# Seven block products in another order, and the weight sums waited for one at a time

## What is computed

```python
x = x + mix @ lp["w_out"]
h = rms_norm(x, lp["norm_ffn"])
x = x + (jax.nn.silu(h @ lp["w_gate"]) * (h @ lp["w_up"])) @ lp["w_down"]
x = x + jax.nn.sigmoid(rms_norm(x, lp["norm_ple"]) @ lp["w_ple_gate"]) * (pe @ lp["w_ple_proj"])
```

## Time and profile before

| | us |
|---|---|
| median of 3 runs | 1913.64 (1911.23 to 1916.33) |
| profiled execution, its own time | 1916.08 |
| span of the profiled execution | 1914.3 |
| PE busy | 1750.2 (91%) |
| DVE busy | 1378.9 (72%) |
| ACT busy | 749.6 (39%) |
| POOL busy | 648.9 (34%) |
| granted TensorE clock, mean | 0.972 |

### The profile page before, as it was taken

One profiled execution on the slowest core, in us unless ns is written; L12 is line 12 of the kernel. 1 busy time (PEld: TensorE's weight loads), 2 busy tenths in 40 slices (PEclk: granted clock), 3 DMA queues, 4 the chain that ended last, 5 costly groups with the idle time before them and its releaser, 6 DMA issues.

```text
span 1914.3 us, 31306 instructions
## 1 busy us (share of the span) xinstructions
PE 1750.2 (91%) x10796; PEld 1522.2 (80%) x10796; DVE 1378.9 (72%) x2307; ACT 749.6 (39%) x1555; POOL 648.9 (34%) x437
## 2 busy tenths in 40 slices
PE   7999899999999989889899999999799998998998
PEld 6998786677888888677788888888588788887777
DVE  5466884765888888655688778877877777676643
ACT  5212455545444444534443334334344344343211
POOL 2204692212554555412622322232334324331000
PEclk9999997999999999999899999999899999999999
DMA  6300000011322222110222312231122312323011
GB/s 204 99 31 16 10 1 1 1 46 44 117 67 64 57 53 80 39 56 1 89 73 81 110 66 80 73 110 66 45 89 88 110 66 89 108 66 137 29 36 47
DMA packets 112122, 126.56 MB, mean 66 GB/s; under 512 B 25923, under 2 KB 98144, under 8 KB 112013
## 3 DMA queue, kind: packets, MB, share of 16 engines
q1 hardware_dynamic: 110019, 124.23, 20.3%
q10 hardware_dynamic: 2002, 1.03, 0.2%
HBM read 119.33 MB, written 6.26 MB: 66 GB/s over the span
## 4 chain that ended last, share of the span: by engine, by line
PE 46%; issue 19%; DVE 16%; POOL 11%; ACT 4%; SPq 3%; DMA 1%; DVEq 0%; POOLq 0%; ACTq 0%
PE ps L2239 11%; PE ps L2240 11%; PE ps L2241 11%; POOL arena L966 2%; POOL stats L813 2%; POOL w_raw L967 2%; POOL arena L969 2%; PE ps L2648 2%; DVE arena L2077 1%; DVE arena L1599 1%; PE ps L569 1%; DVE w_lo L1965 1%; PE ps L2481 1%; DVE arena L2133 1%; SPq L671 1%
## 5 line engine op out<-in xcount | busy, mean ns | idle before, releaser
L2239 PE MATMUL ps<-t_hi,w_hi 128*128 128x288 f32 (+1 forms) x1232 | 359.4, 292 | 13.6 <-DVE arena L2077 6.1
L2241 PE MATMUL ps<-t_hi,w_lo 128*128 128x288 f32 (+1 forms) x1232 | 358.1, 291 | 0.0
L2240 PE MATMUL ps<-t_lo,w_hi 128*128 128x288 f32 (+1 forms) x1232 | 357.9, 290 | 0.0
L2239 PEld LDWEIGHTS ps<-t_hi,w_hi 128*128 128x128 f32 x1232 | 235.3, 191 | 18.5 <-DVE w_lo L1965 6.8
L966 POOL TENSOR_TENSOR arena<-w_raw 128x512 f32<-128x512 f32 x44 | 74.0, 1682 | 501.1 <-DVE w_lo L1965 501.1
L2240 PEld LDWEIGHTS ps<-t_lo,w_hi 128*128 128x128 f32 x1232 | 235.3, 191 | 0.9
L2241 PEld LDWEIGHTS ps<-t_hi,w_lo 128*128 128x128 f32 x1232 | 235.3, 191 | 0.0
L976 POOL TENSOR_TENSOR arena<-arena,mhalf 128x32 f32<-128x32 f32 x32 | 177.1, 5534 | 144.1 <-DVE arena L1978 144.1
L2143 DVE TENSOR_TENSOR arena<-arena,ps 128x512 f32<-128x512 f32 x187 | 127.0, 686 | 112.1 <-PE ps L2241 109.5
L2239 PE MATMUL ps<-wd_hi,a_hi 128*128 128x512 f32 x352 | 148.3, 421 | 36.9 <-DVE wd_lo L2065 26.1
L2239 PE MATMUL ps<-cw_hi,pT_hi 128*128 128x288 f32 x512 | 161.1, 315 | 10.2 <-DVE pT_lo L1880 9.4
(11 more groups left out here) (341 smaller groups left out, 4301.2 us busy)
## 6 DMA issues: line engine op xcount, KB each, us to landing
w_raw<-in_w_gate SPq DMA_DIRECT2D x22, 1024.0 KB, 5.3
w_raw<-in_w_up SPq DMA_DIRECT2D x22, 1024.0 KB, 5.4
arena<-in_cache_ckv SPq DMA_DIRECT2D x128, 128.0 KB, 2.0
w_uk<-in_w_down SPq DMA_DIRECT2D x22, 512.0 KB, 3.5
w_uv<-in_w_down SPq DMA_DIRECT2D x22, 512.0 KB, 4.4
arena<-in_x_prompt SPq DMA_DIRECT2D x16, 512.0 KB, 5.4
gw_raw<-in_w_in SPq DMA_DIRECT2D x8, 512.0 KB, 6.0
w_out<-in_w_out SPq DMA_DIRECT2D x1, 4096.0 KB, 13.4
```

Source lines behind the costliest of these rows:

```text
L2239: mm(out, left[0], right[0], start=start, stop=False)
L2240: mm(out, left[0], right[1], start=False, stop=False)
L2241: return mm(out, left[1], right[0], start=False, stop=stop)
```

## The change

- Products are made in the order 0, 3, 6, 1, 4, 2, 5: the three with plain weight quarters first. PRODUCT_BANK is one table for gate units and another for up units, and PE waits for a bank of the last unit place by place instead of for all of the last unit's sums before its second product.
- POOL waits place by place too: w_diff and the sum in place may start when the low part of quarter 1 of the unit before is made (place 4 of 7), w_back after that of quarter 2 (place 6), w_rest after that of quarter 5 (place 7).
- ACT and DVE follow the new order. Per unit the same 7 high parts, 7 low parts, 7 additions, and per group the same pieces of w_down and of the result are made; only their places move. Both first pieces of w_down come early in the unit, the additions of products 2, 1, 6, 4, 4 and 5 come at its end, and the low part of the first result piece comes before them.
- Result pieces are made by token halves. The down products start after two of the four, and wait for the others before the fifth down product. In half 0 the sample tokens' down product is the fifth and no longer the first, and SP loads the next w_down after the fifth down product and no longer after the first.
- All four token sums of half 0 are made after the loop over the output projection; before, three were made within it. In the last unit of each half all four pieces of w_down are split early.
- Buffers of the split weights and tokens move. The output tiles at the end are taken in the order 4, 5, 6, 7, 0, 1, 2, 3, sample tile, where the sample tile was fifth.

```diff
-DOWN_ORDER = ([(TILES, 0)] + [(t, h) for t in range(4, TILES) for h in range(2)], [(t, h) for t in range(4) for h in range(2)])
+DOWN_ORDER = ([(t, h) for t in (4, 5) for h in range(2)] + [(TILES, 0)] + [(t, h) for t in (6, 7) for h in range(2)], [(t, h) for t in range(4) for h in range(2)])
 DOWNS = [len(o) for o in DOWN_ORDER]
 PRODUCTS = 7
-DONE_AT = {0: 1, 2: 2, 3: 3, 1: 4, 4: 5, 5: 6, 6: 7}
-TOKEN_AT = {0: 1, 3: 2, 1: 3, 2: 4, 4: 5, 5: 6, 6: 7}
-PRODUCT_BANK = {0: 0, 2: 1, 3: 2, 1: 3, 4: 4, 5: 5, 6: 1}
+DONE_AT = {0: 1, 3: 2, 6: 3, 1: 4, 4: 5, 2: 6, 5: 7}
+TOKEN_AT = {0: 1, 3: 2, 1: 3, 6: 4, 4: 5, 2: 6, 5: 7}
+PRODUCT_BANK = ({0: 0, 3: 1, 6: 2, 1: 3, 4: 4, 2: 5, 5: 1}, {0: 0, 3: 5, 6: 2, 1: 3, 4: 4, 2: 1, 5: 5})
+OUT_AT = (((0, 0), 1), ((1, 0), 4), ((1, 1), 5), ((0, 1), 7))
...
-END_TILES = [4, 5, 6, 7, TILES, 0, 1, 2, 3]
+END_TILES = [4, 5, 6, 7, 0, 1, 2, 3, TILES]
...
-                        sp.wait_ge(s_("dn_done"), down_at(0, wd_g) + 1)
+                        sp.wait_ge(s_("dn_done"), down_at(0, wd_g) + 5)
...
-                if isinstance(done, int) and done == 0:
+                first = isinstance(done, int) and done == 0
+                if first:
                     pool.wait_ge(s_("m_xT"), NT)
                 else:
-                    pool.wait_ge(s_("w_split"), PRODUCTS * done)
+                    pool.wait_ge(s_("w_split"), PRODUCTS * (done - 1) + DONE_AT[1])
                 nc.gpsimd.tensor_tensor(w_diff, w_part(u, 0), w_part(u, 4), ALU.subtract).then_inc(s_("w_pool"), 1)
                 nc.gpsimd.tensor_tensor(w_part(u, 4), w_part(u, 4), w_part(u, 6), ALU.add).then_inc(s_("w_pool"), 1)
                 pool.wait_ge(s_("w_pool"), w_sum(c, g, u, 2))
+                if not first:
+                    pool.wait_ge(s_("w_split"), PRODUCTS * (done - 1) + DONE_AT[2])
                 nc.gpsimd.tensor_tensor(w_back, w_part(u, 4), w_part(u, 0), ALU.subtract).then_inc(s_("w_pool"), 1)
                 pool.wait_ge(s_("w_pool"), w_sum(c, g, u, 3))
+                if not first:
+                    pool.wait_ge(s_("w_split"), PRODUCTS * done)
                 nc.gpsimd.tensor_tensor(w_rest, w_part(u, 3), w_back, ALU.subtract).then_inc(s_("w_pool"), 1)
...
-            token_sums(0, (4,))
+            token_sums(0, (1, 2, 3, 4))
...
                 act.wait_ge(s_("prod_done"), PRODUCTS * k + DONE_AT[0])
                 if not first:
-                    act.wait_ge(s_("sum_ready"), 7 * k)
-                    if u == 0:
-                        act.wait_ge(s_("glu_ready"), NU + 4 * (g + GROUPS * c))
-                nc.scalar.activation(p_one[:, 0:n], ps[:, PRODUCT_BANK[0], 0:n], ACT.Copy).then_inc(s_("part_copied"), 1)
-                if following:
-                    high_w(*following, 0)
-                if wd:
+                    act.wait_ge(s_("sum_ready"), 7 * (k - 1) + 2)
+                nc.scalar.activation(p_one[:, 0:n], ps[:, PRODUCT_BANK[u][0], 0:n], ACT.Copy).then_inc(s_("part_copied"), 1)
+                high(0)
+                if wd and len(wd[2]) != 2:
+                    high_wd(*wd)
+                elif wd:
                     high_wd(*wd[0:2], wd[2][0:1])
-                if following:
-                    high_w(*following, 2)
-                    high_w(*following, 3)
+                high(3)
+                if wd and len(wd[2]) == 2:
+                    high_wd(*wd[0:2], wd[2][1:2])
+                silu(0)
+                high(6)
                 if turn is not None:
                     scale_turn(turn)
-                if following:
-                    high_w(*following, 1)
-                silu(0, 0, 2)
-                if wd:
-                    high_wd(*wd[0:2], wd[2][1:2])
-                if following:
-                    high_w(*following, 4)
-                silu(1, 1, 4)
-                if following:
-                    high_w(*following, 5)
-                silu(0, 1, 6)
-                if following:
-                    high_w(*following, 6)
-                silu(1, 0, 7)
-                if u == 1:
-                    if c == 1 and isinstance(g, int) and g == 0:
-                        act.wait_ge(s_("dn_done"), down_at(0, GROUPS))
-                    elif not (c == 0 and isinstance(g, int) and g == 0):
-                        act.wait_ge(s_("dn_done"), down_at(c, g))
-                    for j, (f, h) in enumerate(((0, 0), (1, 1), (0, 1), (1, 0))):
-                        act.wait_ge(s_("glu_ready"), NU + 4 * (g + GROUPS * c) + j + 1)
-                        nc.scalar.activation(a_hi_r[f][:, h * n:(h + 1) * n], gate_s[:, f, h * n:(h + 1) * n], ACT.Copy).then_inc(s_("act_high"), 1)
+                high(1)
+                high_a(0)
+                high(4)
+                high(2)
+                for j in (1, 2):
+                    silu(j)
+                    high_a(j)
+                high(5)
+                silu(3)
+                high_a(3)
...
+                low(0)
+                if wd and len(wd[2]) != 2:
+                    low_wd(*wd)
+                elif wd:
                     low_wd(*wd[0:2], wd[2][0:1])
-                if 0 in gains:
-                    gain_h(*gains[0])
-                dve.wait_ge(s_("part_copied"), k + 1)
                 if not (isinstance(k, int) and k == 0):
                     dve.wait_ge(s_("sum_ready"), 7 * k)
                     dve.wait_ge(s_("glu_ready"), NU + 4 * G)
-                add(p_two, p_one, 2, 1, 0)
-                if following:
-                    low_w(*following, 2)
                 if u == 0 and not first:
                     dve.wait_ge(s_("aT_ready"), 4 * G)
                 if u == 1:
                     dve.wait_ge(s_("silu_ready"), 4 * G + 4)
-                add(out_of(0, 0, p_one), p_one, 3, 2, 1)
-                if following:
-                    low_w(*following, 3)
-                mult(0, 0, p_one, 2)
-                add(p_three, p_two, 1, 3, 1)
-                if following:
-                    low_w(*following, 1)
-                if wd:
+                dve.wait_ge(s_("part_copied"), k + 1)
+                add(out_of(0, c_sum), p_one, 3, 1, 0)
+                low(3)
+                mult(0, c_sum)
+                if wd and len(wd[2]) == 2:
                     low_wd(*wd[0:2], wd[2][1:2])
-                add(out_of(1, 1, c_sum), p_three, 4, 4, 3)
-                add(p_two, p_two, 4, 5, 3)
-                mult(1, 1, c_sum, 4)
-                if following:
-                    low_w(*following, 4)
+                if 0 in gains:
+                    gain_h(*gains[0])
+                low(6)
+                low(1)
+                low_a(0)
+                low(4)
                 if 1 in gains:
                     gain_h(*gains[1])
-                add(out_of(0, 1, p_two), p_two, 5, 6, 5)
-                if following:
-                    low_w(*following, 5)
-                mult(0, 1, p_two, 6)
-                add(out_of(1, 0, p_three), p_three, 6, 7, 4)
-                if following:
-                    low_w(*following, 6)
-                mult(1, 0, p_three, 7)
-                if u == 1:
-                    if c == 0:
-                        dve.wait_ge(s_("glu_ready"), NU + 4 * G + 3)
-                        for f in range(2):
-                            ch.link(nc.vector.tensor_copy(a_s[f], gate_s[:, f, 2 * n - NS:2 * n]))
-                    for j, (f, h) in enumerate(((0, 0), (1, 1), (0, 1), (1, 0))):
-                        dve.wait_ge(s_("act_high"), 2 * NT + 4 * G + j + 1)
-                        w = slice(h * n, (h + 1) * n)
-                        nc.vector.tensor_tensor(a_lo_r[f][:, w], gate_s[:, f, w], a_hi[f][:, w], ALU.subtract).then_inc(s_("aT_ready"), 1)
+                add(p_two, p_one, 2, 2, 0)
+                add(p_three, p_two, 1, 3, 2)
+                if u:
+                    dve.wait_ge(s_("glu_ready"), NU + 4 * G + 1)
+                add(out_of(1, c_sum), p_three, 6, 4, 3)
+                low(2)
+                add(out_of(2, p_three), p_three, 4, 5, 4)
+                mult(1, c_sum)
+                add(p_two, p_two, 4, 6, 3)
+                mult(2, p_three)
+                add(out_of(3, p_two), p_two, 5, 7, 6)
+                low(5)
+                mult(3, p_two)
+                if u == 1 and c == 0:
+                    dve.wait_ge(s_("glu_ready"), NU + 4 * G + 4)
+                    for f in range(2):
+                        ch.link(nc.vector.tensor_copy(a_s[f], gate_s[:, f, 2 * n - NS:2 * n]))
+                for j in (1, 2, 3):
+                    low_a(j)
...
-                if not (fixed and m == 0):
-                    pe.wait_ge(s_("sum_ready"), 7 * (m - 1) + 2)
+                start = fixed and m == 0
+
+                def freed(place):
+                    if not start:
+                        pe.wait_ge(s_("sum_ready"), 7 * (m - 1) + place)
+                if not start:
+                    pe.wait_ge(s_("part_copied"), m)
                 product(0)
                 if turns:
```

(20 more changed lines are left out.)

118 lines of the change are left out of this document (68 added, 50 removed).

## The result

The changed kernel takes **1980.82 us** (median of 4 runs, 1978.62 to 1984.16), the kernel before 1913.2 (1911.23 to 1916.33). The ratio is **1.035, 95% interval 1.033 to 1.038**: slower, as forecast, but by 67.6 us where 36 were forecast, and outside the range of 1888 to 1970.

The account below looks back on a forecast made before the run. Bound: DVE's queue from the up unit's tail to the first down_add, lengthened by POOL. Half 0 +21, half 1 +17.5, start +2, ends -4 make +36.5 on 1916.08: 1952.6, median 2.4 lower, so 1950 us; range 1888 to 1970.

Parts of the forecast that it names:

- term for the clock: Both loops: 12 of 20 stalls followed by a half-clock stretch, at 1.7 us each; 1.0 us per group, 0 to 1.7.
- term for the stall: PE's wait for the first down_add per group: 3.85 us against 2.75 in half 0, 4.65 against 3.9 in half 1.
- The bound: DVE's queue from the up unit's tail to the first down_add, lengthened about 4.3 us by POOL's four sums.
- ideal periods: A group's time from PE's matmuls alone in the kernel before: 35.3 us in half 0, 31.2 in half 1.
- The race with POOL: End of the gate unit: POOL's w_back, first by 0.2 us, holds DVE's low part 5, costing 1.2 us per group.
- rival 1: End of the gate unit: DVE goes first, low part 5 isn't held, 1.2 us less per group; about 1919 us; chance 0.20.
- The blocks in the tail: Up unit's tail: w_back before a multiplication adds 1.0 us to DVE's queue, w_rest before the first copy 1.1.
- Start and ends: Start, before the first down products: +2 us (-3 to +6); ends of the halves: together -4 (0 to -6).
- Rival 2: DVE's queue isn't full, as POOL's earlier sums meet additions and idle time; about 1880 us; chance 0.20.
- Rival 3: PE stalls inside units too, if the up unit's tail is 2 us longer; 1975 to 1990 us; chance 0.05.
- Rival 4: POOL's sums stay held by the loads and the order alone acts; about 1915 to 1930 us; chance 0.05.

Follow-up runs that it names:

- filled kernel: The changed kernel with 16 extra, unread matmuls between the second and third down product of the groups in both loops; 1951.7 us.
- The release of POOL as before: The changed kernel with POOL making its four weight sums again only when all seven low parts of the unit are made; 1980.8 us.

## Why the prediction was right, and where it fell short

The sum failed in the size of its terms and not in its direction. Its term for the clock (12 of 20 stalls followed by a stretch, 1.0 us per group) measured 1.83 and 1.57, with a stretch behind all 19 stalls. Its term for the stall (1.1 and 0.75 us more per group than before) measured 2.2 and 1.5. And the last gate unit of half 0 took 8 us more than forecast, with a wait for ACT in it that the sum put at nothing.

**The bound.** Right for the changed kernel. It named DVE's queue from the up unit's tail to the first down_add, and moving four low parts out of it moved the wait one for one. For the kernel before it was half right: "all of it follows from one date, the end of that down_add" is not so. With 2.4 us taken out ahead of that down_add the periods fell by 1.1 us only, because the last w_down piece, in the same queue but further ahead, was a second date that PE waited for (16.2 us in half 1's loop); only with that piece moved too did they fall by 1.4 and 2.8. The ideal periods were right to 0.3 us. What it undersold is POOL: it gave the four sums 4.3 us of DVE's time in a queue with a loss of 2.75 and 3.9, and did not draw the conclusion that without them nothing would be lost at all.

**The stall.** The mechanism was right, its price too small. Laid out: up unit's tail at 18.8, first down_add done at 28.9, stall 3.85 in half 0. Measured: 19.4, 29.6, and PE goes on 4.06 us later than it could (1057.17 to 1061.23). So the stall itself was nearly right, and what comes on top of it was too small. With the clock held up by the extra matmuls, the period rose by 40.30 - 38.07 = 2.2 in half 0, where 1.1 was forecast, and by 1.5 in half 1, where 0.75 was. Against the kernel before without its sums, which has no wait at all, the filled kernel's down products take 17.44 us and not 13.15 in half 0 (a stall of 4.3, 3.85 laid out), and 15.49 and not 11.30 in half 1 (4.2, as laid out). Its two units take 22.86 and not 22.41 us in half 0, and 21.06 and not 19.98 in half 1: 0.45 and 1.1 of waiting for the first addition, laid out as nothing and 0.5. In half 0 a further 0.25 is the ideal period, 35.3 against 35.56 measured: the 2.75 lost before was counted from it, the 3.85 was not.

One cause can be named. An addition that takes the result of the one just before waits for its semaphore, and starts 0.55 us after it and not 0.37: three take 1.59 us, where 0.45 + 2 x 0.37 = 1.19 was laid out. In half 1 two take 0.94 us, where 0.42 + 0.335 = 0.76 was. The change makes five such pairs per group, together 0.9 us, two of them in the up unit's tail, where they are 0.4 of the 0.6 us by which it was late. In the kernel before other work stands between them. No run undoes this alone.

**The clock.** The other half of the miss in the loops. The prediction let 12 of 20 stalls be followed by 3.4 us at half clock for 1.7 us each, 1.0 per group. No row of before had a stall of 4 us, and 12 of 20 was a guess from waits of 2.4. A stretch followed every stall, and some lasted 6.8 us. By the clock column half 0's loop has 2 x 0.06 x 337.1 = some 40 us at 1.2 GHz in 8 groups (three stretches of 6.8 and five of 3.4 make 37), and the filled wait prices it at 1.83 and 1.57. That is 0.8 and 0.6 per group too little, 12 us in the 17 groups of the loops. The upper end of its range, 1.7 per group, which is a stretch behind every stall, was the right value.

**The last gate unit of half 0.** Put at nothing beyond the stall. From the last down products of the loop to those of the last group it is 51.97 us after and 41.72 before, 10.25 more, of which 2.1 were forecast. ACT in time order, and PE:

```profile
1343.88 0.44 ACT L1471 ACTIVATE a_hi<-gate_s 128x288 fp32r<-128x288 f32 x1 [1.13 <-DVE gate_s L2098]
1344.22 1.13 ACT L1450 ACTIVATE xn_e<-arena,stats 128x1024 f32<-128x1024 f32 x1
```

```profile
1345.50 1.94 PE L570 MATMUL ps<-ident,xn_e 128*128 128x128 f32 x8 [5.42 <-ACT xn_e L1450]
```

PE's next work is the transposition of a token tile that ACT must scale first (scale_turn, L1450). On ACT this stands behind the last result piece (L1471), which waits for DVE's last multiplication, and the up unit's late tail makes that late. PE waits 5.42 us, in the kernel before 1.83. The half clock follows here too: the transposition takes 1.94 against 1.06. The prediction followed ACT's queue for the weights and never asked what stands in it behind the last result piece outside the loops. Of the 8 us too many, 2.0 are what each group of half 0's loop also lost beyond the forecast, 3.6 are the longer wait, and some 2.5, by estimate, the 5 us at half clock behind it. This is read from the trace; no run moved that scaling.

**The race with POOL.** The prediction hung 1.2 us per group, and its rival 1, on whether w_back holds low part 5. Neither happened: low part 5 waited for ACT, w_back started at 1058.57 beside an addition, and low part 5 ran at 1059.88 in 0.69 us. POOL held low part 2 instead, 1.54 us in place of 0.69. The blocks in the tail were as laid out: a multiplication of 1.40 us, the two copies 1.40 together. The release of POOL as before shows that this bookkeeping was the wrong level: take a block from one place and most of it lands in the next., on which rival 1 leaned, lacks the DVE row ahead of the sum:

```profile
1404.05 0.41 DVE L2087 TENSOR_TENSOR gate_s<-gate_s,arena 128x256 f32<-128x256 f32 x1
```

This multiplication reads two SBUF operands too and was already running when POOL's sum was issued at 1404.21. So the sum was not first there.

**Start and ends.** Right in size; no run tests their parts. From the first product to the first down products it is 50.80 us against 48.07, +2.7 (forecast +2). The end of half 0 gave back 3.9 (55.6 to 51.7), the very end 1.4 (15.7 to 14.3), together 5.3 where 4 was forecast.

**The sum.** Forecast 21 + 17.5 + 2 - 4 = 36.5, measured 71.9 in the feed-forward part. By place the missing 35 are 8 x (4.06 - 2.1) + 9 x (3.03 - 1.75) = 27 in the loops, 8 in the last gate unit of half 0, 2.5 in the last group of half 1 (26.7 to 30.9, 4.2 more where 1.75 was forecast), less 2 in the rest: the tenth group of half 0 has no stall (37.3 us before, 37.5 after), where 2.1 was forecast. By cause the loops' 27 are 12 of clock and 15 of stall and unit waits (8 x 1.1 + 9 x 0.7).

**The rivals.** Rival 2 (the queue is not full) is false even without POOL's sums, where 1.4 and 2.1 us of wait remain. DVE's work fits into the group, but six of seven additions cannot start before the sixth product is done. Rival 3, stalls inside units as well, is in part what half 1 shows, and its 1975 to 1990 holds the time, though by another way: the tail was 0.6 us late and not 2. It had 0.05, and the range left it out. Rival 4 (loads hold POOL's sums) shows nowhere.

## What to carry to other kernels

When PE waits once per group for a queue on another engine, first ask what in that queue PE doesn't need yet, and move it behind; moving four 0.6 us instructions past the first addition took 25 us off the kernel before and 93 off the changed one. An order that makes six of seven consumers wait for a late product leaves the consumer idle early and late at the end, even when its busy time is unchanged. And price a recurring stall with the half-speed stretch behind it: here a stall of 4 us cost 5.8 in half 0's loop.
